# Fetching the rows of two expert tables in turn, and making a block's weights ahead of a later block's selection

## The chip, the cores and the metric

One core of a Trainium2 chip runs one inference step of a small diffusion backbone. The metric is the device time of one execution in microseconds (us). The engines have the profile's names: PE (matrix multiply), DVE (vector), ACT (scalar functions), POOL (here it only issues row fetches), SP (issues the other loads).

## The reference, cut to what matters

384 tokens of width 1024 (128 context tokens, "prompt", and 256 noisy ones, "sample") pass two layers. Layer 0 mixes with an RG-LRU, layer 1 with gated linear attention (GLA). After either comes PEER, a mixture of 16384 tiny experts for each layer, which is where most of the time goes:

```python
def peer(xm, wq, k1, k2, u_tab, v_tab):
    ...
    v1, i1 = lax.top_k(s1, PEER_TOPK)          # 16 of 128 keys, in 8 heads
    v2, i2 = lax.top_k(s2, PEER_TOPK)
    cand = (v1[..., :, None] + v2[..., None, :]).reshape(T, PEER_HEADS, -1)
    cid = (i1[..., :, None] * PEER_NKEYS + i2[..., None, :]).reshape(T, PEER_HEADS, -1)
    sc, pos = lax.top_k(cand, PEER_TOPK)       # 16 experts a head and token
    eid = jnp.take_along_axis(cid, pos, axis=-1)
    gate = jax.nn.softmax(sc, axis=-1)
    ...
        ub = jnp.take(u_tab, eb, axis=0)
        act = jax.nn.gelu(jnp.einsum('td,thkd->thk', xb, ub).astype(jnp.float32))
        vb = jnp.take(v_tab, eb, axis=0)
        return jnp.einsum('thk,thkd->td', (gb * act).astype(vb.dtype), vb)
```

Everything is fp32. For each token and head, 16 rows of 4 KB are taken from the first table (u) and dotted with the token, and 16 rows of the second table (v) are summed with weights gate x gelu(dot).

## The kernel before, in words

The kernel is written with explicit semaphores: each engine runs its own instruction list in order, and every wait is placed by hand or by a table.

**Blocks and rows.** PEER is cut into 48 blocks of 128 tokens and one head: for layer 0 sixteen sample blocks (numbers 0 to 15) and eight prompt blocks (16 to 23), for layer 1 the same (24 to 39, 40 to 47). A block has 16 fetches of each table. One fetch is one `indirect_dma_start` on POOL: it takes 128 table rows of 4 KB, one for each token, to one slot of a ring (512 KB). Below, "row" means such a fetch. The ring of the first table, `ubuf`, has US = 8 slots, that of the second, `vbuf`, VS = 12.

**What happens to a row.** DVE multiplies a first-table row with the tokens and sums it to one column of `dots` (line 1331, a "dot"); this frees the slot (`u_free`). After 16 dots DVE makes the inner value of the gelu (1337 to 1339), ACT its tanh (669), and DVE the weights `wts` (1345 to 1351). ACT turns each column of weights to a diagonal matrix (677), and PE multiplies that with the second-table row and adds to PSUM (974); this frees the slot (`v_free`).

**Selection.** DVE also selects the 16 experts of a block two blocks ahead: `row_tops` (the 16 best of either 128 keys) and `choose` (16 of the 256 sums, and their row numbers `idx`, with a flag at line 1177 on which POOL waits). In a block the order on DVE is: 16 dots, inner value, `row_tops(g + 2)`, weights, `choose(g + 2)`.

**POOL's queue.** The order is written out in two loops. A fetch of the first table waits until the dot eight rows earlier has freed its slot, one of the second until PE has used the row twelve earlier:

```python
            for g, (layer, h, t) in enumerate(BLOCKS):
                ...
                for j in range(TOPK):
                    n = g * TOPK + j
                    if n >= US:
                        pool.wait_ge(u_free, n - US + 1)
                    pool.indirect_dma_start(
                ...
                for j in range(TOPK):
                    n = g * TOPK + j
                    if n >= VS:
                        pool.wait_ge(v_free, n - VS + 1)
```

**The mixers between.** Sample tokens finish layer 0's PEER with block 15, prompt tokens with block 23, so the sample's GLA mixer of layer 1 runs beside the prompt's blocks 16 to 23, and the prompt's mixer beside blocks 24 to 39. The mixers are cut into stages on PE, ACT and DVE. The table `AT` says for each engine and stage after which row (PE: 16 places a block; ACT: 18; DVE: 20) the stage is inserted into the engine's list: a string of turns (S sample, P prompt, Q the PEER queries and scores, T early selections) and a list of places. Slabs of GLA weights (1 MB) come on SP's queue through two buffers. A stage that waits holds up everything behind it on its engine, the rows too.

Of the kernel before, what the change touches and what calls it, by code (L numbers as in the profile page):

```python
# [30 lines left out]
US, VS, DS = 8, 12, 8  # L31
# [39 lines left out]
class Stream:  # L71


    def __init__(self, tag, w, a, n, rot, rot_end):
# [36 lines left out]
        for step in plan:  # L111
# [18 lines left out]
        "QQQQQQQQQQQQSSSSSSSSSSSSSSSSSSSSSSSSSSSSSSSSSSSSSSSSSSSSSSSSSSSSSSSSSSSSSSSSSSSSSQQQQQQQQPPPPPPPQPQP"  # L130
        "PPPPPPPPPPQPPQPPPPPPPPPPPPPPPQPPQPPPPPQPQPPQQQQQQQQQQSSSSQSQQQQQPPP",
# [8 lines left out]
    "ACT": (  # L140
        "SQQQQQQQQQQQQSSSSSSSSSSSSSSSSSSSSSSSSSSSSSSSSSSSSSSSSSSSPQQQQQQQPPPPPPPPQQPPPPPPPQQPPPPPQQPPPPQPQPPP"
        "PQQQQQQQQQQSSQSSSQSQQQQQPPPP",
# [54 lines left out]
def build(nc, x_t, pos_t, vecs, ident_d, mask_d, iota_d, keys_t, ada_w, peer_wq, peer_u, peer_v, rg_w_in,  # L197
          rg_wa, rg_wi, rg_w_out, gla_w_in, w_alpha, state_gla, gla_w_out, y_t, st_rg, st_gla):
    ctx = ExitStack()
    with ctx:  # L200
# [235 lines left out]
        def _(pool):  # L436
# [7 lines left out]
            for g, (layer, h, t) in enumerate(BLOCKS):  # L444
                if t == 0:
                    pool.wait_ge(sem("idx_p"), PH * layer + h + 1)
                else:
                    pool.wait_ge(sem("idx_s"), 2 * PH * layer + 2 * h + t)
# [1044 lines left out]
```

## Time and profile before

| | us |
|---|---|
| three runs, median (lowest to highest) | 2939.15 (2932.97 to 2952.03) |
| the profiled execution, its own time | 2934.96 |
| its span, first to last instruction | 2933.2 |
| PE busy | 2168.3 |
| POOL busy | 1634.3 |
| DVE busy | 1585.9 |
| ACT busy | 538.7 |

The profile is of one execution. Busy time is the time in which an engine works on instructions; idle time stands in front of the instruction that it had to wait for, with what ended the wait. The mean granted clock of PE was 0.862 of full speed. The lines that the prediction rests on come below in numbered groups.

### The profile page before, as it was taken

What the parts mean: (1) busy time and instruction counts of PE and PEld (TensorE: products, weight loads), DVE (VectorE), ACT (ScalarE), POOL (GpSimd) and SP (SyncE); (2) the same over time, 40 slices, a digit from 0 to 9 for tenths busy, and PEclk for the clock granted to TensorE, in tenths of its full rate; (3) what the DMA queues carried; (4) which work ended last, traced back from release to release, by engine and by line L of the source; (5) the groups of instructions that cost most, each with busy time, mean ns of one, the idle gap of its engine ahead of it and who ended that gap; (6) DMA issues with size and microseconds to landing.
All of it is one profiled execution on the core that took longest, in us unless ns stands there. A gap on an engine that the chain in (4) does not pass through costs nothing.

```text
span 2933.2 us, 22324 instructions
## 1 busy us (share of the span) xinstructions
PE 2168.3 (74%) x6996; PEld 1147.8 (39%) x6996; DVE 1585.9 (54%) x3991; ACT 538.7 (18%) x1376; POOL 1634.3 (56%) x1543
## 2 busy tenths in 40 slices
PE   6989667687774747988796697867957576558666
PEld 2545333233332324856442265334524233223323
DVE  3253667666767545164525445665564774466553
ACT  2432111111110113221211122111211111111111
POOL 0000767675767764053567554767575767475664
PEclk9999888898897878988898798888978787778888
DMA  9990989999999996476799788989898999799996
GB/s 307 311 326 16 372 337 361 357 387 339 366 367 361 360 368 237 142 281 225 270 364 379 288 325 315 362 307 347 316 371 311 370 361 363 271 335 345 348 385 245
DMA packets 352933, 938.66 MB, mean 320 GB/s; under 512 B 32369, under 2 KB 155505, under 8 KB 352305
## 3 DMA queue, kind: packets, MB, share of 16 engines
q0 software_dynamic: 221184, 805.40, 73.0%
q1 hardware_dynamic: 123184, 125.32, 13.2%
q10 hardware_dynamic: 8448, 6.51, 0.7%
q8 instruction: 58, 0.95, 0.1%
q14 instruction: 59, 0.48, 0.0%
HBM read 934.49 MB, written 2.63 MB: 319 GB/s over the span
## 4 chain that ended last, share of the span: by engine, by line
PE 34%; another core or an unknown queue 16%; POOL 16%; DMA 12%; issue 12%; DVE 9%; ACT 1%; ACTq 1%; SPq 0%; DVEq 0%; POOLq 0%
PE psum L974 18%; POOL big L454 13%; DMA big<-in_peer_u,idx 4%; PE psum L859 4%; DVE big L1331 3%; POOL big L461 3%; PE psum L797 3%; PE psum L818 3%; DMA big<-in_gla_w_in 2%; DMA big<-in_peer_wq 2%; DMA big<-in_peer_v,idx 2%; PE psum L899 1%; DMA big<-in_ada_w 1%; PE psum L762 1%
## 5 line engine op out<-in xcount | busy, mean ns | idle before, releaser
L974 PE MATMUL psum<-big,diag 128*128 128x512 f32 x3072 | 1435.7, 627 | 485.8 <-issue 244.1
L1331 DVE SCALAR_TENSOR_TENSOR big<-big 128x1024 f32<-128x1024 f32 x768 | 929.9, 1225 | 605.2 <-DMA big<-in_peer_u,idx 526.5
L454 POOL DMA_INDIRECT big<-in_peer_u,idx x768 | 859.4, 1119 | 594.7 <-DVE flag L1177 287.5
L461 POOL DMA_INDIRECT big<-in_peer_v,idx x768 | 770.8, 1004 | 676.8 <-PE psum L974 424.4
L974 PEld LDWEIGHTS psum<-big,diag 128*128 128x128 f32 x3072 | 611.7, 202 | 1264.9 <-issue 1262.8
L677 ACT ACTIVATE diag<-ident,wts 128x128 f32<-128x128 f32 x768 | 273.6, 395 | 914.1 <-PE psum L974 531.9
L818 PE MATMUL psum<-big 128*128 128x384 f32 (+2 forms) x768 | 186.1, 405 | 55.3 <-DMA big<-in_peer_wq 41.6
L818 PEld LDWEIGHTS psum<-big 128*128 128x128 f32 x768 | 136.6, 206 | 112.6 <-DMA big<-in_peer_wq 47.2
L859 PE MATMUL psum<-big 128*128 128x256 f32 (+1 forms) x768 | 142.0, 347 | 42.9 <-issue 19.9
L859 PEld LDWEIGHTS psum<-big 128*128 128x128 f32 x768 | 127.0, 206 | 60.6 <-issue 48.7
L669 ACT ACTIVATE tanh<-inner 128x16 f32<-128x16 f32 x48 | 10.3, 214 | 703.5 <-DVE inner L1339 389.4
L797 PE MATMUL psum<-big 128*128 128x384 f32 x384 | 130.2, 496 | 7.2 <-DVE big L1411 5.2
L797 PEld LDWEIGHTS psum<-big 128*128 128x128 f32 x384 | 72.6, 193 | 61.6 <-issue 11.4
L1194 DVE SCALAR_TENSOR_TENSOR xT<-psum,mods,xT 128x256 f32<-128x256 f32 (+1 forms) x48 | 16.9, 410 | 121.3 <-PE psum L869 98.6
L525 ACT ACTIVATE big<-psum 128x384 f32<-128x384 f32 (+2 forms) x48 | 18.2, 384 | 276.7 <-PE psum L818 187.7
L762 PE MATMUL psum<-big,cond 128*2 128x256 f32 x768 | 52.1, 393 | 19.7 <-DMA big<-in_ada_w 19.7
L1331 DVE DVE_READ_ACCUMULATOR big<-big 128x1 f32 x768 | 62.7, 82 | 0.0
L830 PE MATMUL psum<-big 128*128 128x128 f32 x192 | 28.9, 293 | 40.1 <-ACT big L525 32.6
L1246 DVE COPY big<-psum 128x512 f32<-128x512 f32 (+1 forms) x8 | 4.5, 556 | 96.7 <-PE psum L899 69.7
L869 PE MATMUL psum<-ident,big 128*128 128x128 f32 x48 | 10.2, 395 | 61.7 <-ACT big L568 61.7
L899 PE MATMUL psum<-big 128*128 128x256 f32 x192 | 44.1, 390 | 10.2 <-DMA big<-in_gla_w_in 10.0
L830 PEld LDWEIGHTS psum<-big 128*128 128x128 f32 x192 | 26.8, 204 | 50.0 <-issue 49.2
(182 smaller groups left out, 1306.5 us busy)
## 6 DMA issues: line engine op xcount, KB each, us to landing
big<-in_ada_w SPq DMA_DIRECT2D x48, 1024.0 KB, 8.4
big<-in_peer_wq SPq DMA_DIRECT2D x24, 1024.0 KB
big<-in_gla_w_in SPq DMA_DIRECT2D x24, 1024.0 KB
big<-in_peer_u,idx POOLq DMA_INDIRECT x768
big<-in_peer_v,idx POOLq DMA_INDIRECT x768
big<-in_rg_w_in SPq DMA_DIRECT2D x8, 1024.0 KB, 12.1
big<-in_gla_w_out SPq DMA_DIRECT2D x8, 1024.0 KB
big<-in_rg_w_out SPq DMA_DIRECT2D x4, 1024.0 KB, 8.3
```

What stands on the lines that cost most here:

```text
L454: pool.indirect_dma_start(ubuf[n % US], None, u_rows, bass.IndirectOffsetOnAxis(ap=rows[:, j:j + 1], axis=0)).then_inc(u_in[n % US], 16)
L461: pool.indirect_dma_start(vbuf[n % VS], None, v_rows, bass.IndirectOffsetOnAxis(ap=rows[:, j:j + 1], axis=0)).then_inc(v_in[n % VS], 16)
L525: act.activation(qT[w][half], bank[6 + half][:, 0:width], ACT.Copy).then_inc(sem("q_ev"), 1)
L677: act.activation(diag[n % DS][:, :], ident[:, :], ACT.Copy, scale=wts[g % 3][:, j:j + 1]).then_inc(sem("diag_ready"), 1)
L762: mm = pe.matmul(out[32 * s:32 * s + 2, o:o + SW], cond[:, c, :], slab[SLOT[k]][:, c, :], start=False, stop=(c == C - 1), skip_group_check ...
L797: mm = pe.matmul(out, slab[SLOT[k]][:, c, (n % 2) * P:(n % 2 + 1) * P], rhs[:, c, :], start=(c == 0), stop=(c == C - 1))
L818: mm = pe.matmul(bank[6 + half][:, 0:width], weights[:, c, half * P:(half + 1) * P], rhs[:, c, :], start=(c == 0), stop=(c == C - 1))
L830: mm = pe.matmul(bank[6 + half][:, t * P:(t + 1) * P], qT[w][half][:, t * P:(t + 1) * P], table[:, o:o + NK], start=True, stop=True)
L859: mm = pe.matmul(out[:, j * n:(j + 1) * n], weights[:, c, j % 2 * P:(j % 2 + 1) * P], rhs[:, c, :], start=(c == 0), stop=(c == C - 1), ski ...
L899: mm = pe.matmul(out[:, t * DV:(t + 1) * DV], s.hT[:, c, t * P:(t + 1) * P], weights[:, c, :], start=(c == 0), stop=(c == C - 1), skip_gro ...
L974: mm = pe.matmul(acc[t][:, half * 512:(half + 1) * 512], diag[n % DS][:, :], vbuf[n % VS][:, half * 512:(half + 1) * 512], start=False, st ...
L1331: dve.scalar_tensor_tensor(ubuf[n % US], ubuf[n % US], 1.0, x, ALU.mult, ALU.mult, accum_out=dot[:, j:j + 1]).then_inc(u_free, 1)
```

## The change

Both rings get 10 slots, in place of 8 for the first table and 12 for the second. POOL's queue first takes all 16 rows of the first table for block 0; then, row for row, a row of the second table for block g and one of the first table for block g + 1. On DVE the weights of a block are made directly after its inner value, and `row_tops` of the later block comes behind them. The factor 0.5 of the gelu goes into the dot, so that the two steps ahead of the last one of the weights (scale by the reciprocal sum, multiply by the dots) become one instruction. The places in `AT` are new throughout: on PE the sample's GLA projections, which stood together behind one row (place 268), are now spread over places 267 to 284, and the steps after them over 294 to 321 (before 277 to 304); on DVE the sample's state steps, which stood in one place (379), are spread over 397 to 409; the prompt's stages are spread likewise.

```diff
-US, VS, DS = 8, 12, 8
+US, VS, DS = 10, 10, 8
...
-            for g, (layer, h, t) in enumerate(BLOCKS):
-                if t == 0:
-                    pool.wait_ge(sem("idx_p"), PH * layer + h + 1)
-                else:
-                    pool.wait_ge(sem("idx_s"), 2 * PH * layer + 2 * h + t)
-                rows = idx[kept(g)]
+
+            def first_table(g, j):
+                n = g * TOPK + j
+                if j == 0:
+                    layer, h, t = BLOCKS[g]
+                    if t == 0:
+                        pool.wait_ge(sem("idx_p"), PH * layer + h + 1)
+                    else:
+                        pool.wait_ge(sem("idx_s"), 2 * PH * layer + 2 * h + t)
+                if n >= US:
+                    pool.wait_ge(u_free, n - US + 1)
+                pool.indirect_dma_start(
+                    ubuf[n % US], None, u_rows,
+                    bass.IndirectOffsetOnAxis(ap=idx[kept(g)][:, j:j + 1], axis=0)).then_inc(u_in[n % US], 16)
+
+            def second_table(g, j):
+                n = g * TOPK + j
+                if n >= VS:
+                    pool.wait_ge(v_free, n - VS + 1)
+                pool.indirect_dma_start(
+                    vbuf[n % VS], None, v_rows,
+                    bass.IndirectOffsetOnAxis(ap=idx[kept(g)][:, j:j + 1], axis=0)).then_inc(v_in[n % VS], 16)
+
+            for j in range(TOPK):
+                first_table(0, j)
+            for g in range(NBLK):
                 for j in range(TOPK):
...
+                    second_table(g, j)
+                    if g + 1 < NBLK:
+                        first_table(g + 1, j)
...
-                act.activation(tanh[g % 2][:, :], inner[g % 2][:, :], ACT.Tanh, scale=GELU_C
+                act.activation(tanh[g % 2][:, :], inner[g % 2][:, :], ACT.Tanh, scale=2 * GELU_C
...
-                    dve.scalar_tensor_tensor(ubuf[n % US], ubuf[n % US], 1.0, x, ALU.mult, ALU.mult,
+                    dve.scalar_tensor_tensor(ubuf[n % US], ubuf[n % US], 0.5, x, ALU.mult, ALU.mult,
                                              accum_out=dot[:, j:j + 1]).then_inc(u_free, 1)
...
-                link(dve.tensor_scalar(inn[:, :], inn[:, :], 0.044715, 1.0, ALU.mult, ALU.add))
+                link(dve.tensor_scalar(inn[:, :], inn[:, :], 4 * 0.044715, 1.0, ALU.mult, ALU.add))
                 dve.tensor_tensor(inn[:, :], inn[:, :], dot[:, :], ALU.mult).then_inc(sem("inner_ready"), 1)
                 stages(slot + 17)
-                if look:
-                    row_tops(ahead)
-                stages(slot + 18)
                 dve.wait_ge(sem("exp_ready"), g + 1)
                 link(dve.reciprocal(rz[:, :], esum[r][:, :]))
-                link(dve.tensor_scalar(sc[r][:, :], sc[r][:, :], rz[:, 0:1], 0.5, ALU.mult, ALU.mult))
-                link(dve.tensor_tensor(sc[r][:, :], sc[r][:, :], dot[:, :], ALU.mult))
+                link(dve.scalar_tensor_tensor(sc[r][:, :], sc[r][:, :], rz[:, 0:1], dot[:, :], ALU.mult, ALU.mult))
                 dve.wait_ge(sem("tanh_ready"), g + 1)
                 if g >= 3:
                     dve.wait_ge(sem("diag_ready"), (g - 2) * TOPK)
                 dve.scalar_tensor_tensor(wts[g % 3][:, :], tanh[g % 2][:, :], 1.0, sc[r][:, :], ALU.add, ALU.mult
                                          ).then_inc(sem("w_ready"), 1)
+                stages(slot + 18)
+                if look:
+                    row_tops(ahead)
                 stages(slot + 19)
```

## Rows read from the trace of the kernel before

**Rows 1.** The page: span, and the queue of the row fetches.

```profile
span 2933.2 us, 22324 instructions
...
q0 software_dynamic: 221184, 805.40, 73.0%
```

**Rows 2.** The page's groups: out<-in, count | busy us, mean ns | idle before.

```profile
L974 PE MATMUL psum<-big,diag 128*128 128x512 f32 x3072 | 1435.7, 627 | 485.8 <-issue 244.1
L1331 DVE SCALAR_TENSOR_TENSOR big<-big 128x1024 f32<-128x1024 f32 x768 | 929.9, 1225 | 605.2 <-DMA big<-in_peer_u,idx 526.5
L454 POOL DMA_INDIRECT big<-in_peer_u,idx x768 | 859.4, 1119 | 594.7 <-DVE flag L1177 287.5
L461 POOL DMA_INDIRECT big<-in_peer_v,idx x768 | 770.8, 1004 | 676.8 <-PE psum L974 424.4
```

**Rows 3.** POOL's waits over the span: us, times, longest.

```profile
POOL big L461 <- PE psum L974: 424.4, 171, 82.9
POOL big L454 <- DVE flag L1177: 287.5, 3, 286.8
...
POOL big L454 <- DVE big L1331: 76.4, 13, 13.4
POOL big L461 <- remote: 63.1, 31, 5.3
```

**Rows 4.** Stretches: length; busy PE, PEld, DVE, ACT, POOL; clock, DMA share, GB/s.

```profile
291.00:1076.00 785.00, 562.64 (x1318) 257.67 (x1316) 528.15 (x1467) 112.87 (x334) 547.97 (x525) 0.85 0.95 360
1076.00:1554.00 478.00, 392.82 (x1456) 260.96 (x1456) 204.50 (x412) 102.25 (x219) 215.28 (x194) 0.88 0.73 262
1554.00:1646.00 92.00, 60.63 (x128) 26.07 (x128) 40.80 (x78) 12.54 (x38) 65.10 (x67) 0.81 0.97 373
1646.00:2128.00 482.00, 376.64 (x1344) 219.51 (x1344) 267.40 (x696) 98.23 (x252) 290.89 (x256) 0.87 0.88 321
2128.00:2516.00 388.00, 262.60 (x692) 126.81 (x692) 228.21 (x598) 54.57 (x172) 268.40 (x255) 0.83 0.95 358
2516.00:2907.00 391.00, 247.09 (x624) 116.96 (x625) 211.01 (x527) 58.71 (x178) 242.64 (x243) 0.80 0.90 336
...
820.00:840.00 20.00, 18.33 (x43) 7.79 (x41) 7.74 (x13) 1.20 (x3) 15.02 (x17) 1.00 1.03 412
...
1180.00:1240.00 60.00, 60.00 (x279) 52.82 (x278) 13.64 (x12) 11.17 (x10) 0.00 (x0) 1.00 0.50 157
```

**Rows 5.** POOL's timeline, the longest wait for a ring slot: start, length.

```profile
1244.54 0.95 POOL L461 DMA_INDIRECT big<-in_peer_v,idx  x1 [82.92 <-PE psum L974]
```

**Rows 6.** Timeline of block 10: issues that begin inside a dot.

```profile
793.47 1.99 POOL L454 DMA_INDIRECT big<-in_peer_u,idx  x1 [0.30 <-issue]
794.57 1.22 DVE L1331 SCALAR_TENSOR_TENSOR big<-big 128x1024 f32<-128x1024 f32 x1
...
795.72 1.22 DVE L1331 SCALAR_TENSOR_TENSOR big<-big 128x1024 f32<-128x1024 f32 x1
795.76 1.99 POOL L454 DMA_INDIRECT big<-in_peer_u,idx  x1 [0.30 <-issue]
```

**Rows 7.** Timeline of block 11: its first fetch and dot, and issues beside dots.

```profile
825.85 0.94 POOL L454 DMA_INDIRECT big<-in_peer_u,idx  x1 [0.30 <-issue]
...
832.04 1.28 DVE L1331 SCALAR_TENSOR_TENSOR big<-big 128x1024 f32<-128x1024 f32 x1 [12.56 <-DMA big<-in_peer_u,idx]
...
833.31 0.94 POOL L454 DMA_INDIRECT big<-in_peer_u,idx  x1 [0.31 <-issue]
833.33 1.24 DVE L1331 SCALAR_TENSOR_TENSOR big<-big 128x1024 f32<-128x1024 f32 x1
```

**Rows 8.** DVE's timeline of block 10, from the last dot to the flag.

```profile
809.68 0.17 DVE L1337 TENSOR_TENSOR inner<-dots 128x16 f32<-128x16 f32 x1
...
813.33 0.17 DVE L1351 SCALAR_TENSOR_TENSOR wts<-tanh,sc 128x16 f32<-128x16 f32 x1
...
819.42 0.06 DVE L1177 MEMSET flag<- 128x1 f32 x1
```

More of the change, by code:

```diff
@@ L129 @@
     "PE": (
-        "QQQQQQQQQQQQSSSSSSSSSSSSSSSSSSSSSSSSSSSSSSSSSSSSSSSSSSSSSSSSSSSSSSSSSSSSSSSSSSSSSQQQQQQQQPPPPPPPQPQP"
-        "PPPPPPPPPPQPPQPPPPPPPPPPPPPPPQPPQPPPPPQPQPPQQQQQQQQQQSSSSQSQQQQQPPP",
[8 rows of a table removed]
-    "ACT": (
-        "SQQQQQQQQQQQQSSSSSSSSSSSSSSSSSSSSSSSSSSSSSSSSSSSSSSSSSSSPQQQQQQQPPPPPPPPQQPPPPPPPQQPPPPPQQPPPPQPQPPP"
-        "PQQQQQQQQQQSSQSSSQSQQQQQPPPP",
[6 rows of a table removed]
+        "QQQQQQQQQQQQSSSSSSSSSSSSSSSSSSSSSSSSSSSSSSSSSSSSSSSSSSSSSSSSSSSSSSSSSSSSSSSSSSSSSQQQQQQQQPPPPPPPQQPP"
+        "PPPPPQQPPPPPPPPPPPPPPPPPPPPPPPPPPPQQPPPPPQQQQQQQQQQQQSSSSQQSQQQQPPP",
[8 rows of a table added]
+    "ACT": (
+        "SQQQQQQQQQQQQSSSSSSSSSSSSSSSSSSSSSSSSSSSSSSSSSSSSSSSSSSSPQQQQQQQPPPPPPPQPQPPPQPPQPPPPPPPPPPQQPPPPPPQ"
+        "QQQQQQQQQQQSQQSSSSSQQQQQPPPP",
[6 rows of a table added]
          864]),
@@ L443, in _ @@
             pool.wait_ge(sem("h_ready"), 32)
-            for g, (layer, h, t) in enumerate(BLOCKS):
-                if t == 0:
-                    pool.wait_ge(sem("idx_p"), PH * layer + h + 1)
-                else:
-                    pool.wait_ge(sem("idx_s"), 2 * PH * layer + 2 * h + t)
-                rows = idx[kept(g)]
-                for j in range(TOPK):
-                    n = g * TOPK + j
-                    if n >= US:
-                        pool.wait_ge(u_free, n - US + 1)
-                    pool.indirect_dma_start(
-                        ubuf[n % US], None, u_rows,
-                        bass.IndirectOffsetOnAxis(ap=rows[:, j:j + 1], axis=0)).then_inc(u_in[n % US], 16)
-                for j in range(TOPK):
-                    n = g * TOPK + j
-                    if n >= VS:
-                        pool.wait_ge(v_free, n - VS + 1)
-                    pool.indirect_dma_start(
-                        vbuf[n % VS], None, v_rows,
-                        bass.IndirectOffsetOnAxis(ap=rows[:, j:j + 1], axis=0)).then_inc(v_in[n % VS], 16)
+            def first_table(g, j):
[21 more added lines that the diff above has]
+            for g in range(NBLK):
+                for j in range(TOPK):
+                    second_table(g, j)
+                    if g + 1 < NBLK:
+                        first_table(g + 1, j)
         @block.scalar
```

38 rows, old and new, of the table AT are left out of this document.

## The prediction

> **What bounds the kernel now.** I read the page's groups first, then POOL's waits, then the stages, and only then single instructions. The groups [rows 2] name two candidates. PE spends 1435.7 us on the weighted rows of the second table, 1.87 us a row; POOL spends 859.4 + 770.8 us on issuing the 1536 row fetches, and idles 594.7 + 676.8 us in front of them. Of that idle time 287.5 us lie ahead of the first fetch and 424.4 + 76.4 + 63.1 = 563.9 us are waits for a free ring slot [rows 3]; the remaining 420 us are the 0.30 us step in front of nearly every issue [rows 7]. So from 291 us to 2907 us POOL is either issuing (some 80% of the time) or waiting for a slot, and it is never idle for another reason. The fetches are one queue in program order, so this ledger is the time of the main loop.
>
> The ledger by stage, from the six stretches of [rows 4]: an issue costs 0.94 us when nothing disturbs it [rows 7], plus 0.30, so 32 of them (one block) cost 39.7 us. What a stretch has beyond 1.24 us times its count is disturbance of the issue (POOL's busy time less 0.94 times the count) or a stall.
> - A, 291 to 1076: 525 issues (16.4 blocks), 47.8 us a block: 39.7 + 3.3 slow + 4.8 stall.
> - B, 1076 to 1554, in which the sample's second mixer runs: 194 issues, 204 us of stall.
> - C, 1554 to 1646: 67 issues, 44 us a block, 1.0 of it slow.
> - D, 1646 to 2128, the prompt's mixer: 256 issues, 114 us of stall, 6.3 us slow a block.
> - E, 2128 to 2516: 255 issues, 48.7 us a block, 3.6 slow. F, 2516 to 2907: 243 issues, 51.5 us a block, 1.9 slow.
>
> Is a transfer limit close behind? The fetches move 805.40 MB [rows 1], 16.78 MB a block; the best stretches move 412 GB/s at a share of 1.03 [rows 4], so a block alone needs 40.7 us. With the other loads, the DMA time of a stage is its length times its share: A 0.95 x 785 = 746 us, and at 1.03 it could not be under 724. The same for C, D, E, F: 87, 412, 358, 342. In B PE is the floor instead, with 392.8 us busy of 478 [rows 4].
>
> **What the change does to each.**
> *Order of the fetches.* Before, the queue was sixteen of the first table, sixteen of the second; the thirteenth of the second waits until PE has used the block's first row, which needs the block's weights, which need all sixteen dots. Everything of the next block is queued behind it. After, row j of the second table stands beside row j of the next block's first table, and either ring has 10 slots. The second table's eleventh row is then 21 issues (26 us) behind the last row on which its weights depend. That row lands 6.2 us after its issue starts [rows 7], its dot takes 1.2 [rows 7], the weights follow within 4 [rows 8], and a row of PE 1.9 [rows 2]: 13 us, so 13 us are spare. The next block's eleventh first-table row waits for a dot that starts after the choice of a later block: 6.2 + 1.2 + 9.7 (from the first step after the dots to the flag, [rows 8]) + 1.2 = 18 us against 27. So in plain blocks neither wait should bind, and I leave 0.5 us a block of the 4.8 for the odd late row. The same 32 fetches are issued; nothing is added.
>
> *Weights ahead of the selection.* The row tops lie between the inner value and the weights; both together take 3.65 us from 809.68 to 813.33 [rows 8]. Moving them and merging two 16-element operations brings the weights at most 3 us earlier. The merged step (a few tenths of a us of DVE) is worth nothing by itself, since DVE waits for rows; if that cover were gone it would be 0.2 us in each of 48 blocks, 10 us. The new place adds one wait: DVE now stands until the tanh is back, with the row tops queued behind it, and POOL's next index behind them. ACT's tanh is short and the spare 9 us above cover it; in the mixer stages, where ACT can be late, it may cost something, which I leave in those stages' own range.
>
> *The disturbed issue.* This is the term that decides the plain blocks. Where a fetch is issued just after a dot has begun (795.76 against 795.72), the issue lasts 1.99 us and ends 0.8 us after that dot's end; the next starts 2.29 us after, two dots later, and meets the same thing again [rows 6]. Where issue and dot begin together the issue takes 0.94 and the dots merely stretch to 1.28 and 1.24 [rows 7]. Before, only the first table's issues run beside dots. After, all 32 do. The bounds a block: 1.0 us, as in stage C, and 16 x 1.05 = 16.8 us, every dot delaying one issue by the most that is seen. My value: the choice holds the dots back 9.7 us, so about four rows wait, and with those in flight some 6 dots run back to back; at one issue per two dots that is 3 issues late by 1.05, 3.1 us. The other 10 dots start when their row lands; a random phase would cost half a dot (0.6), a favourable one nothing; 0.3 each, 3.0 us. Together 6.1, close to what stage D pays.
>
> The Trainium skill, "SBUF — State Buffer", section "SBUF: two separate sides", says that a VectorE instruction with two SBUF inputs and a GpSimd instruction that reads SBUF exclude one another for a whole instruction, whichever starts first. The late issues agree with it in one direction [rows 6]; the undisturbed pairs [rows 7] show that the lock is not held for the whole issue. By the rule taken strictly each dot would cost one issue between nothing and its full 1.22 us, at the mean 9.8 us a block in place of 6.1, and the sum would be 2922 us; the slower rival below is this with more than the mean.
>
> *Plain blocks* after: 39.7 + 6.1 + 0.5 = 46.3 us, above the transfer floor of A (724 / 16.4 = 44.1). A 760 (-25), C 97 (+5), E 369 (-19), F 7.6 x 46.3 + 15 for the final transposes of the sample rows, inside which DVE waits, 366 (-25): -64 us.
>
> *Stage B.* The longest stall, 82.9 us [rows 5], is PE: it works through the projections without a pause (60 of 60 us, DMA at 0.50, [rows 4]). The new order of PE puts two or three weighted rows between pairs of slabs, so the fetches go on under the projections; the work of PE stays. At best 85 us, to PE's floor. But the steps after them hold PE at row 299 until DVE is some 20 to 26 rows further on, which is about the most that the rings allow (26), and there each further row costs an issue and 6.2 us of landing, one after the other. I take half: -40. *Stage D*: between 412 and 482; DMA is shared with slabs and the order is again spread; half: -35. Start and end (291 and 27 us) have the same chain before and after, the last sixteen rows of PE behind the last weights: nothing.
>
> Sum: -64 - 40 - 35 = -139. The profiled execution took 2934.96 us, 0.14% under the median of 2939.15, so **2796 us**, 4.8% less.
>
> **The rivals.**
> *It reaches the floors.* If dots and issues fall into step as in [rows 7], each stage ends on DMA or PE: -61 in A, -5, -70, -30, -49, and -85 in B, 300 together: 2635 us. For it: DMA at 0.95 in A is near. Against: stage D, where most dots meet issues, pays 6.3 us.
> *Nothing is gained.* If all 16 dots run back to back against the issues (8 issues late by 1.05, 8.4 us), a block costs 48.6 us, which is the mean of A, C, E and F now (1656 us for 34.1 blocks); with a quarter of the gain in B and D, 2916 us. For it: the ring waits that vanish may only have been standing in for disturbed issues. Also here: the queue is one, so a stop of PE in the mixers now stops the first table after ten rows of the second, as it did after twelve.
> *Slower: dots shut POOL out.* Place: the plain blocks. Price: a delay for each dot, with two issues now offered to each. It decides from the point where 34.1 blocks lose the 75 us won in B and D: 48.6 + 2.2 = 50.8 us a block, 10.6 us of delay, 0.66 us a dot. At 0.85 us a dot a block takes 39.7 + 13.6 + 0.5 = 53.8 us: +177 - 75, 3037 us. For it: late issues come in runs, as in [rows 6]. Against: the dots fill only 929.9 / 48 = 19.4 us of a block [rows 2], and pause for 9.7 of it.
> *The change doesn't do what it says*: the weights are not early enough and the second table still stalls at its eleventh row. The 13 us spare speak against it in plain blocks; it would look like the rival without gain.
>
> **How the numbers follow.** Forecast (2735 to 2870) 0.48; floors 0.22; nothing gained 0.15; slower 0.15. A change under 1% can't be told from none here (the three runs before differ by 0.65%). Faster by over 1% means under 2910: nearly all of the first two and a third of the third, 0.74; within 1% 0.13; slower 0.13. Leaving out the best part of the floors and the worst of the slower cases, the range is 2650 to 2960.
>
> **What would show it.** POOL's waits for PE and for the dots should fall from 564 us to about 300, nearly all of that left in B and D. The means of the two fetch groups should rise from 1119 and 1004 ns towards some 1130 each, the second table's most. The longest single stall should be well under 80 us, and DMA in A reach 0.97 to 1.0. If the means exceed 1270 ns, the slower rival holds; if stalls in A remain at 4 us a block, the slots were not what held it. The forecast fails too if the mixers' new order makes PE and DVE wait on one another, which would stand in B and D alone.

## The result, and the profile after

The changed kernel took 2922.53 us in the median of 20 runs beside 2941.47 us of 20 runs of the kernel before: a ratio of 0.9918, with a 95% interval of 0.9890 to 0.9945. A ratio, here and below, is formed from the runs within 1.5% of the fastest of their kernel, so it can differ from that of the two medians. The forecast was 2796 us. By its time, what came is the rival "nothing is gained", which stood at 2916.

The page's span and groups of the changed kernel answer to [rows 1, 2]; the dot has moved to L1341, the two fetches to L455 and L463, PE's rows to L984:

```profile
span 2908.3 us, 22245 instructions
...
L984 PE MATMUL psum<-big,diag 128*128 128x512 f32 x3072 | 1495.0, 628 | 392.6 <-DMA big<-in_peer_v,idx 245.3
L1341 DVE SCALAR_TENSOR_TENSOR big<-big 128x1024 f32<-128x1024 f32 x768 | 914.3, 1223 | 668.1 <-DMA big<-in_peer_u,idx 587.0
L455 POOL DMA_INDIRECT big<-in_peer_u,idx x768 | 856.6, 1115 | 676.7 <-DVE flag L1187 290.8
L463 POOL DMA_INDIRECT big<-in_peer_v,idx x768 | 892.3, 1162 | 454.2 <-PE psum L984 232.5
```

POOL's waits over the span, beside [rows 3]:

```profile
POOL big L455 <- DVE flag L1187: 290.8, 1, 290.8
POOL big L463 <- PE psum L984: 232.5, 122, 22.1
...
POOL big L455 <- DVE big L1341: 157.8, 19, 18.4
POOL big L463 <- remote: 28.0, 14, 4.9
```

So the second table's wait for PE fell from 424.4 to 232.5 us, as meant; the first table's wait for the dots doubled, from 76.4 to 157.8; and POOL's issues took 1748.9 us in place of 1630.2. Ring waits less 146, issues more 119: 27 us, against 24.9 us by which the span fell.

The stretches, with the columns of [rows 4] and cut at the same six stages:

```profile
295.00:1172.00 877.00, 605.30 (x1305) 242.83 (x1304) 519.38 (x1458) 109.98 (x334) 601.12 (x526) 0.90 0.86 323
1172.00:1570.00 398.00, 358.81 (x1386) 238.09 (x1385) 203.47 (x406) 101.40 (x212) 216.51 (x192) 0.94 0.85 304
1570.00:1665.00 95.00, 79.14 (x199) 36.50 (x197) 40.48 (x75) 13.73 (x42) 72.51 (x66) 0.96 1.03 396
1665.00:2112.00 447.00, 368.79 (x1321) 219.01 (x1322) 260.07 (x686) 102.19 (x254) 295.22 (x256) 0.90 0.93 343
2112.00:2512.00 400.00, 291.46 (x720) 125.39 (x718) 224.08 (x594) 53.01 (x172) 284.99 (x256) 0.91 0.93 353
2512.00:2885.00 373.00, 270.44 (x643) 114.28 (x644) 200.18 (x511) 59.86 (x184) 278.60 (x242) 0.93 0.93 350
```

Against the forecast of each stage: B 398 (438 forecast), C 95 (97), D 447 (447), F 373 (366). A took 877 where 760 was forecast, and E 400 where 369 was; A is even 92 us longer than before. The plain blocks (A, C, E, F) miss by 153 us and B gives 40 back, 113 over the six. Of A's waits 113.4 us, in nine waits, are the first table's eleventh row that waits for a dot; in E and F together it is 44.4 us, in ten:

```profile
POOL big L455 <- DVE big L1341: 113.4, 9, 18.4
...
POOL big L455 <- DVE big L1341: 30.2, 5, 8.9
...
POOL big L455 <- DVE big L1341: 14.2, 5, 6.2
```

The longest of them follows block 9. VectorE's timeline there, then POOL's (start, length, operation, and in brackets the idle time before it; DVE_READ_ACCUMULATOR and the steps without a pause are left out):

```profile
819.32 0.17 DVE L1357 SCALAR_TENSOR_TENSOR wts<-tanh,sc 128x16 f32<-128x16 f32 x1
...
821.83 0.29 DVE L1141 MAX8 v<-work 128x8 f32<-128x128 f32 x1 [0.71 <-DVE v L1141]
823.26 0.09 DVE L1144 MATCH_VALUE_LOAD i12u<-v,work 128x8 f32 x1 [1.14 <-issue]
...
824.65 0.09 DVE L1144 MATCH_VALUE_LOAD i12u<-v,work 128x8 f32 x1 [1.03 <-issue]
...
830.28 0.42 DVE L1161 TENSOR_TENSOR cand<-v 128x256 f32<-128x256 f32 x1 [5.26 <-remote]
...
831.68 0.43 DVE L1133 MAX8 sc<-cand 128x8 f32<-128x256 f32 x1 [0.81 <-issue]
835.26 0.09 DVE L1136 MATCH_VALUE_LOAD posu<-sc,cand 128x8 f32 x1 [3.16 <-remote]
...
838.76 0.43 DVE L1141 MAX8 sc<-onehot 128x8 f32<-128x256 f32 x1 [2.62 <-remote]
...
842.68 0.06 DVE L1187 MEMSET flag<- 128x1 f32 x1
...
850.89 0.06 DVE L1187 MEMSET flag<- 128x1 f32 x1
```

```profile
833.07 0.93 POOL L463 DMA_INDIRECT big<-in_peer_v,idx  x1 [0.30 <-issue]
852.37 1.67 POOL L455 DMA_INDIRECT big<-in_peer_u,idx  x1 [18.36 <-DVE big L1341]
```

Two things are to be seen. There are two flags: the table of places puts the early selection of a later block (the T stages) at the end of every odd block of the first layer, right behind the ordinary one. And the first selection takes 23.4 us, from 819.3 to 842.7, the second, of the same steps, 8.2 us. What makes the first long is seven idle times, 14.7 us together, in front of steps that, by the code, wait for a semaphore of a step before them on the same engine (one of the seven, at 831.68, stands behind a wait for PE too, which had ended by 830.30). The pause between block 9's last dot (its end at 818.30) and the next one (850.87) is 32.6 us; without the seven it is 17.8. The late steps lie where the fetches go out back to back and their rows land (the last issue before POOL's wait starts at 833.07, the last late step at 838.76); the second selection runs while POOL stands still. Late loading of code is not seen: the two queues that carry instructions move nothing between 815 and 855 us.

The other pauses agree. Less its idle times over 0.3 us, the pause behind an odd block up to 13 is 17.5 to 18.3 us, and behind an even one up to 12 it is 9.3 to 9.6; those idle times add 9.3 to 18.4 us to every one of the seven doubled pauses, mainly to the first selection in four of them and to the second in three. Seven of A's nine waits, 98.2 us, stand behind these. The other two, 15.2 us, follow blocks 2 and 4, which have one selection, with 14.2 and 15.6 us of late steps; and no pause in front of the ten waits of E and F holds a T stage. So 59.7 of the 157.8 us stand behind single selections with late steps.

### The profile page after: what moved, and what is told of

Read it like the earlier page. It is cut to its first block, busy times and chain, and to the rows that moved or that the text cites. A ratio compares the mean times of both kernels' runs of the same rounds, so it can differ in the third digit from the quotient of the medians.

```text
span 2908.3 us, 22245 instructions
## 1 busy us (share of the span) xinstructions
PE 2240.7 (77%) x6996; PEld 1118.9 (38%) x6996; DVE 1553.6 (53%) x3943; ACT 539.3 (19%) x1379; POOL 1752.9 (60%) x1543
## 4 chain that ended last, share of the span: by engine, by line
PE 27%; POOL 21%; DMA 15%; issue 13%; DVE 12%; another core or an unknown queue 11%; ACT 1%; ACTq 1%; SPq 0%; DVEq 0%; POOLq 0%
PE psum L984 11%; POOL big L455 11%; POOL big L463 10%; DMA big<-in_peer_v,idx 5%; DMA big<-in_peer_u,idx 5%; PE psum L869 4%; PE psum L807 3%; PE psum L828 3%; DMA big<-in_peer_wq 2%; DVE big L1341 2%; DMA big<-in_ada_w 2%; PE psum L909 1%; PE psum L772 1%; DMA big<-in_gla_w_out 1%
## 5 line engine op out<-in xcount | busy, mean ns | idle before, releaser
L984 PE MATMUL psum<-big,diag 128*128 128x512 f32 x3072 | 1495.0, 628 | 392.6 <-DMA big<-in_peer_v,idx 245.3
L1341 DVE SCALAR_TENSOR_TENSOR big<-big 128x1024 f32<-128x1024 f32 x768 | 914.3, 1223 | 668.1 <-DMA big<-in_peer_u,idx 587.0
L455 POOL DMA_INDIRECT big<-in_peer_u,idx x768 | 856.6, 1115 | 676.7 <-DVE flag L1187 290.8
L463 POOL DMA_INDIRECT big<-in_peer_v,idx x768 | 892.3, 1162 | 454.2 <-PE psum L984 232.5
L984 PEld LDWEIGHTS psum<-big,diag 128*128 128x128 f32 x3072 | 570.8, 197 | 1259.1 <-issue 763.5
L828 PE MATMUL psum<-big 128*128 128x384 f32 (+2 forms) x768 | 209.4, 441 | 137.2 <-ACT big L550 85.9
L828 PEld LDWEIGHTS psum<-big 128*128 128x128 f32 x768 | 151.3, 229 | 204.5 <-issue 148.5
L869 PEld LDWEIGHTS psum<-big 128*128 128x128 f32 x768 | 127.4, 207 | 50.7 <-issue 24.2
L807 PEld LDWEIGHTS psum<-big 128*128 128x128 f32 x384 | 74.7, 197 | 62.4 <-issue 14.5
L1341 DVE DVE_READ_ACCUMULATOR big<-big 128x1 f32 x768 | 62.6, 82 | 0.0
L1141 DVE MAX8 sc<-onehot 128x8 f32<-128x256 f32 x48 | 20.5, 428 | 66.6 <-remote 44.3
L1161 DVE TENSOR_TENSOR cand<-v 128x256 f32<-128x256 f32 x48 | 21.3, 444 | 47.4 <-remote 32.4
L909 PEld LDWEIGHTS psum<-big 128*128 128x128 f32 x192 | 39.7, 208 | 18.2 <-issue 12.2
L1179 DVE TENSOR_TENSOR onehot<-ab,iota 128x512 f32<-128x512 f32 x48 | 33.2, 692 | 15.1 <-DVE ab L1175 7.3
```

The lines of the kernel that those rows point to most:

```text
L455: pool.indirect_dma_start(ubuf[n % US], None, u_rows, bass.IndirectOffsetOnAxis(ap=idx[kept(g)][:, j:j + 1], axis=0)).then_inc(u_in[n % US ...
L463: pool.indirect_dma_start(vbuf[n % VS], None, v_rows, bass.IndirectOffsetOnAxis(ap=idx[kept(g)][:, j:j + 1], axis=0)).then_inc(v_in[n % VS ...
L807: mm = pe.matmul(out, slab[SLOT[k]][:, c, (n % 2) * P:(n % 2 + 1) * P], rhs[:, c, :], start=(c == 0), stop=(c == C - 1))
L828: mm = pe.matmul(bank[6 + half][:, 0:width], weights[:, c, half * P:(half + 1) * P], rhs[:, c, :], start=(c == 0), stop=(c == C - 1))
L869: mm = pe.matmul(out[:, j * n:(j + 1) * n], weights[:, c, j % 2 * P:(j % 2 + 1) * P], rhs[:, c, :], start=(c == 0), stop=(c == C - 1), ski ...
L909: mm = pe.matmul(out[:, t * DV:(t + 1) * DV], s.hT[:, c, t * P:(t + 1) * P], weights[:, c, :], start=(c == 0), stop=(c == C - 1), skip_gro ...
```

## The experiments

The theories, as the expectations number them: **1**, semaphores that come late stretch the selection until ten rows of the ring don't cover the pause; **2**, the doubled selection alone does that; **3**, the gain is lost to issues that last longer beside two-input dots. "Blocks 0 to 15" below is the time from the first dot of block 0 to that of block 16, read from the timeline: 764.8 us before, 838.2 after; blocks 16 to 23 take 568.0 and 493.7. A ratio is to the kernel before, run beside it; kernels without one had a single run, and the 20 runs of the changed kernel lie between 2896 and 2946 us.

**Half rows.** The same fetches, at half the bytes; PE uses the half row for both halves of its sum, and the dot is scaled by 0.05.

```diff
-u_rows = peer_u.rearrange("l n d -> (l n) d")
+u_rows = peer_u.rearrange("l n (two d) -> (l n two) d", two=2)
-ubuf[n % US], None, u_rows,
+ubuf[n % US][:, 0:D // 2], None, u_rows,     # likewise for the second table
```

> The changed kernel, but each fetch brings half a row (2 KB in place of 4 KB a partition), from other rows of the tables; dots and weighted rows keep their widths and work partly on old data, the dot scaled by 0.05. Same number of fetches, same instructions on every engine. Theory 1 (under a saturated DMA the semaphores come late, the selection's chain of short VectorE steps grows from 6 to 9.5 us and the eleventh first-table row waits): with DMA at half its share the choice falls back to 6.0 to 6.5 us, VectorE's gaps inside chained steps fall from 293 to under 60 us, the waits of the first table for dots in the first stage fall from 113 to under 40 us; total 2740 to 2820 us. Theory 2 (the second selection after every odd block is too long by its work alone): these waits stay above 70 us, after odd blocks only; total 2840 to 2900. Theory 3 (issues disturbed by dots eat the gain): fetch means stay at 1115 and 1162 ns and the time stays within 2870 to 2920.

> The kernel before with the same half rows (data and scale of the dot changed in the same way). Its selection is already 6 us long, so Theory 1 expects little in VectorE's gaps (79 us to under 40), and the second table's waits for PE to fall only by what a row lands sooner (about 1 to 3 us a block, 50 to 120 us): 2820 to 2890 us, so that the change is worth 60 to 100 us at half rows in place of 25. Theory 2 and Theory 3: both kernels gain alike, and the difference between the two stays at 20 to 40 us.

Measured: 2760.9 us for the changed kernel, 2858.5 for the one before: between these single runs the change is worth 98 us, in place of 19 between the medians at whole rows. POOL's waits in the first:

```profile
POOL big L463 <- PE psum L984: 164.1, 190, 11.8
POOL big L455 <- DVE big L1341: 27.6, 7, 8.6
```

The idle times over 0.3 us inside the selections, added up over the trace, fell from 293 us to 87 (in the kernel before from 79 to 71), and the choice from 10.6 to 7.5 us. Theory 1 had the total and the waits for dots right, but wanted under 60 us of late steps and a choice of 6.0 to 6.5. POOL's issues grew to 1840.6 us, 92 more. It is theory 1's side; but a half row also lands sooner, and the late steps were not gone, so the pair half_again and half_spread below was added.

**A sum in place of the dot.** One SBUF input in place of two, and one column written in place of a whole row; 1.21 us in place of 1.22.

```diff
-dve.scalar_tensor_tensor(ubuf[n % US], ubuf[n % US], 0.5, x, ..., accum_out=dot[:, j:j + 1])
+dve.tensor_reduce(dot[:, j:j + 1], ubuf[n % US], AX_X, ALU.add)
```

> The changed kernel with each dot replaced by a plain sum over the fetched row: one input from SBUF and no product with the token (so that part of the computation is left out). Theory 3 (what the change wins is lost to fetch issues that last longer beside two-input dots): the fetch means fall from 1115 and 1162 ns to 940 to 1000, some 250 us less on GpSimd, and the total to 2650 to 2750 us. Theories 1 and 2: the issues may get as short, but the time goes into ring waits, since DMA (0.93 in the first stage) and the selection set the pace: 2800 to 2900 us, and the waits for dots and PE grow from 418 us by more than 100.

> The kernel before with the same plain sum in place of the dot (the product with the token is left out). Theory 3: here only the first table's issues were disturbed (1119 ns), so it gains at most 16 x 0.18 us a block, 130 us: 2800 to 2860, and the change is worth over 100 us between the two kernels with sums. Theories 1 and 2: the change stays worth under 50 us between them.

Measured: 2795.4 and 2956.2 us, so that the change is worth 161 us. The fetches of the changed kernel with sums:

```profile
L463 POOL DMA_INDIRECT big<-in_peer_v,idx x768 | 728.1, 948 | 707.9 <-PE psum L984 390.7
L455 POOL DMA_INDIRECT big<-in_peer_u,idx x768 | 731.3, 952 | 597.8 <-DVE flag L1187 287.1
```

The issues are at their undisturbed 0.95 us, so what lengthens them is the dot's instruction; whether by its second input or by the row that it writes, this edit doesn't separate. POOL's busy time falls by 289 us, the ring waits grow from 418 to 608, the span falls by 115. In the kernel before the same edit takes 181 us from POOL and gives nothing: its wait for PE grows from 424.4 to 581.1 us. Neither side has all its numbers. Theory 3 had the issue times and the worth of over 100 us right, but both totals wrong (2795.4 against 2650 to 2750, 2956.2 against 2800 to 2860). Theories 1 and 2 had the growth of the waits right and the first total nearly (2800 to 2900), and were wrong on the worth, which they put under 50 us. The price of the disturbed issue already stands in the forecast (6.1 us a block; 6.4 measured). It is a cost of the new order, and not the one that was missed; the next three runs show that.

**The pause taken apart.** "spread" moves the T stages from slots 40, 80, ... 280 (the ends of blocks 1, 3, ... 13) to 48, 88, ... 288 (behind the eighth dot of the next block), and the query projections that they hold up by four places on PE and up to two on ScalarE. "mid" moves the row tops:

```diff
 for j in range(TOPK):
     ... dot j ...
+    if look and j == 11:
+        row_tops(ahead)
     stages(slot + 1 + j)
 ...
 stages(slot + 18)
-if look:
-    row_tops(ahead)
 stages(slot + 19)
```

> The changed kernel with the early selections of blocks 16 to 22 moved from the end of the odd blocks of layer 0 (where each stands right behind another selection) to the middle of the block after (behind its eighth dot), with the query projections that they hold up moved along by a few places. Same instructions. Theories 1 and 2 (the doubled pause of the dots is longer than the ten rows of the first ring cover): the waits of the first table for dots in the first stage fall from 113 us to under 40, the sixteen first blocks take 765 to 800 us in place of 838, total 2850 to 2885 us. Theory 3 (issues beside dots): waits that vanish come back as longer issues, since the dots then run back to back less often but the same issues stay disturbed: total within 2900 to 2930.

> The changed kernel with the row tops of the selection (MAX8 and its like on the scores, some 3.7 us) moved from the end of the block to between its eleventh and its twelfth dot plus one; the rest of the selection stays. Theory 1 (a chain of short steps that gets long under a saturated DMA, so that its length decides): the pause between the blocks' dots falls by 4 to 8 us, the waits for dots by a third to a half: 2860 to 2895 us. Theory 2 alone: only the odd blocks of layer 0 gain, 7 times 4 to 5 us: 2885 to 2900. Theory 3: no change, 2905 to 2930.

> Both of these edits in one kernel. Theories 1 and 2: the waits of the first table for dots all but vanish (under 40 us of 158), total 2820 to 2865 us. Theory 3: within 2890 to 2930.

Measured: spread 2835.8 us, ratio 0.9708 [0.9619, 0.9797]; mid 2833.1, 0.9717 [0.9621, 0.9812]; both 2781.5, 0.9545 [0.9452, 0.9638]. Blocks 0 to 15 take 772.3, 813.8 and 775.5 us. POOL's waits of spread, then those of mid for dots, and then of spread_mid with its groups of fetches:

```profile
POOL big L463 <- PE psum L984: 252.6, 131, 19.6
...
POOL big L455 <- DVE big L1341: 66.1, 16, 9.0
```

```profile
POOL big L455 <- DVE big L1343: 72.0, 9, 12.1
```

```profile
POOL big L463 <- PE psum L984: 227.7, 130, 16.6
...
POOL big L455 <- DVE big L1343: 31.1, 9, 8.9
POOL big L463 <- remote: 23.1, 10, 5.2
POOL big L463 <- DVE big L1343: 4.0, 1, 4.0
```

```profile
L455 POOL DMA_INDIRECT big<-in_peer_u,idx x768 | 886.2, 1154 | 553.6 <-DVE flag L1187 291.2
L463 POOL DMA_INDIRECT big<-in_peer_v,idx x768 | 866.6, 1128 | 446.0 <-PE psum L984 227.7
```

In spread_mid POOL's issues are as long as in the changed kernel (1752.8 against 1748.9 us), the ring waits fell from 418 to 286 us, and the span by 127: the gain is in the waits. The first table's wait for dots is 66.1 us with the second selection moved away, close to the 59.7 that stood behind single selections, 72.0 in mid, and 31.1 with both. Theory 3 expected 2890 or more for all three and falls as the explanation of the miss. On this chip the kernel before was faster, too (2925.0 us); by their ratios the three would be at 2856, 2858 and 2808 us beside the 2941.47 above. So spread is where theories 1 and 2 put it; mid is at the lower edge of theory 1's range and well under the 2885 to 2900 of theory 2 alone; and the two together are some 12 us better than expected. Fewer steps were late, too (145 us in place of 293).

The time of spread_mid is near the forecast, but its parts are not. Blocks 0 to 15, at 775.5 us, are no shorter than in the kernel before (764.8), where the forecast had 25 us off in A. What it wins lies in blocks 16 to 23 (478 us in place of 568) and 24 to 39 (809 in place of 871). Its stretch that answers to A is as long as A was, with the same share of DMA:

```profile
295.00:1080.00 785.00, 579.40 (x1297) 242.06 (x1296) 503.84 (x1438) 111.81 (x334) 583.31 (x517) 0.92 0.95 357
```

**The weights alone.**

> The kernel before (its order of fetches, rings of 8 and 12, places) with one part of the change: the block's weights are made ahead of the selection, with the two 16-element operations merged. As the prediction has it, the weights come 3 us earlier and shorten the second table's wait at its thirteenth row in the plain blocks by up to that: 0 to 60 us off, 2880 to 2940. The rival, that the wait for the tanh costs as much as the move gives: 2935 to 2955. If it alone reaches 2920, the new order of the fetches is worth nothing as it stands.

Measured: 2915.6 us, ratio 0.9944 [0.9890, 0.9999]; the wait of L461 for PE fell from 424.4 to 332.6 us, and that for the dots rose from 76.4 to 115.1:

```profile
POOL big L461 <- PE psum L974: 332.6, 139, 78.5
...
POOL big L454 <- DVE big L1331: 115.1, 18, 13.3
```

Alone it wins 0.6%, with an interval that all but touches 1, where the whole change wins 0.8% (1.2% in the comparison further below). The intervals overlap: that the new order, with its rings and places, adds anything as it stands is not shown.

**The old order with the pause taken apart, and the new order with the old places.** The first is weights_only with the edits of spread_mid (T stages on the same slots, PE's query places moved by four); the second puts the table of the kernel before into the changed one.

> The kernel before (sixteen of the first table, then sixteen of the second; rings of 8 and 12; its places) with the weights ahead of the selection and with both edits of the run spread_mid: early selections in the middle of the block after, row tops behind the twelfth dot. Theory A (the new order lets the next block's fetches pass the wait for the weights, and its gain was only covered by the pause of the dots): the old order gains little from shorter pauses, its second table still waits for the weights: 2880 to 2915 us, at least 80 us over spread_mid. Rival B (the pause of the dots is all there was, and either order gains alike): 2780 to 2850 us.

> The changed kernel with the table of places of the kernel before (when PE, ScalarE and VectorE turn to the mixers and the query projections); the order of the fetches, the rings and the early weights are those of the change. If the new places are what made the sample's mixer 59 us shorter (blocks 16 to 23: 552 to 494 us), these blocks take 530 us or more and the total is 2945 to 2985 us. If the order of the fetches did it, the total stays within 2900 to 2940 us; the first sixteen blocks stay at 820 to 850 us in either case.

Measured: 3014.7 us, ratio 1.0150 [1.0072, 1.0229], and 3033.4 us, 1.0340 [1.0287, 1.0393]. The first ratio rests on two of six runs, of 2964.4 and 2994.2 us; the trace is of one of 3011.2. POOL's waits of the old order taken apart, then of the new order at the old places:

```profile
POOL big L461 <- PE psum L974: 450.6, 166, 78.2
...
POOL big L454 <- DVE big L1333: 94.6, 14, 13.3
```

```profile
POOL big L455 <- DVE big L1341: 362.8, 38, 41.1
...
POOL big L463 <- PE psum L984: 158.9, 108, 74.6
```

The old order loses with the edit that wins 4% in the new one: the row tops now stand ahead of the last four dots, the weights come later, and the second table's thirteenth row waits for them (332.6 to 450.6 us). So the two orders want opposite things of VectorE: the old one the weights early, the new one short pauses. Theory A expected no gain there (2880 to 2915) and met a loss. The old places cost the new order more than the 2945 to 2985 expected: blocks 16 to 23 take 532.7 us, near the threshold of 530, but 24 to 31 also 39 us more than in the changed kernel, and blocks 0 to 15 take 862.3, over the 820 to 850 expected in either case. The expectation's "552" for the kernel before was misread; it is 568.0, so the new places and order together win 74 us there, not 59. The old order with the new places was not run, so how much of this the places would win by themselves stays open.

**Further apart, and a shorter ring.** "all_mid" puts the row tops behind the eighth dot, the choice behind the twelfth, the T stages behind the fourth; "ring_9_10" sets `US, VS = 9, 10` in the changed kernel.

> The changed kernel with the selection taken apart further: row tops behind the eighth dot, the choice behind the twelfth, the early selections of blocks 16 to 22 behind the fourth dot of the even blocks, so that only the weights stand between two blocks' dots. If the pause of the dots still costs ring waits (31 us for the first table in spread_mid) and the rest is late weights behind the choice, 2745 to 2780 us. If spread_mid already stands at the transfers (DMA at 0.94 to 0.98 in its plain stages): within 1% of it, 2770 to 2800 us.

> The changed kernel with 9 rows in the first table's ring in place of 10. The dose of Theory 1 and 2: a pause that ten rows do not cover costs one row more, two issues of 1.15 + 0.3 us, 2.9 us each time: the 23 waits of the first table for dots and about as many that ten rows just covered, some 45 times 2.9: +60 to +130 us, 2980 to 3050 us, nearly all in the plain blocks. If the waits have to do with issues or places instead: within 20 us of the changed kernel.

Measured: 2800.7 us, ratio 0.9545 [0.9493, 0.9597], the same as spread_mid: taking the pause apart further won nothing more. The shorter ring: 2929.0 us, 0.9999 [0.9964, 1.0035], and its wait for dots:

```profile
POOL big L455 <- DVE big L1341: 182.4, 20, 17.9
```

That is 0.8% over the change, some 24 us (by the intervals 10 to 37), and 182.4 us of waits for dots in place of 157.8. The expectation, 60 to 130, missed; the other side, within 20, is nearer. The number of waits stayed at 20 (19 in the changed kernel, where the expectation has 23), so no waits came up that ten rows had just covered. Blocks 0 to 15 take 857.9 us, 20 more, as seven odd blocks at 2.9 us would have it; but another execution of the changed kernel (change_again) took 852.9 there, so that is no support. A ring that fills earlier also ends the run of issues earlier, and with it the late steps (262 us in place of 293); that this is why the dose is small was not tested.

**What the doubled pause costs by itself.** Half rows again, with and without the edit of spread, and the changed kernel and spread_mid on one chip.

> The run half_after once more, timed in rounds beside half_spread (half rows, the dot scaled by 0.05): 2750 to 2775 us, with the waits of the first table for dots at 20 to 40 us.

> Half rows (as in half_after: each fetch brings half a row, other rows of the tables, the dot scaled by 0.05) together with the early selections in the middle of the block after (as in spread). If the doubled pause and the late semaphores cost only together (two selections of 8.6 us each just fit under the ten rows' cover when their steps are not late), moving the second selection gives little at half rows: within 25 us of half_again. If the doubled pause costs by itself, it gives as much as at whole rows, 60 to 90 us: 2670 to 2700 us.

> The changed kernel itself, on the chip on which spread_mid is timed again: 2905 to 2930 us, a ratio to the kernel before of 0.989 to 0.996. All theories expect the same; it gives the distance between the two on one chip.

> The run spread_mid once more, beside the changed kernel: 2775 to 2815 us, a ratio to the kernel before of 0.945 to 0.964, and 100 to 140 us under the changed kernel, if the pause of the dots is what ate the change's gain.

Measured: half_again 2760.3 us, 0.9479 [0.9436, 0.9522]; half_spread 2733.5, 0.9387 [0.9357, 0.9417]. The edit is worth 27 us at half rows (12 to 42 by the intervals), just over the 25 of the first reading and far from the second's 60 to 90, and at whole rows (0.9918 to 0.9708) some 60 (34 to 89). Block 5's pause in half_again:

```profile
573.53 0.17 DVE L1357 SCALAR_TENSOR_TENSOR wts<-tanh,sc 128x16 f32<-128x16 f32 x1
...
581.86 0.06 DVE L1187 MEMSET flag<- 128x1 f32 x1
...
588.45 0.43 DVE L1141 MAX8 sc<-onehot 128x8 f32<-128x256 f32 x1 [2.31 <-remote]
...
590.55 0.17 DVE L1173 TENSOR_SCALAR abu<-posu 128x16 uint32<-128x16 uint32 x1 [1.15 <-DVE posu L1144]
...
594.75 0.69 DVE L1182 TENSOR_TENSOR onehot<-onehot,i 128x512 f32<-128x512 f32 x1 [2.10 <-issue]
...
597.58 0.06 DVE L1187 MEMSET flag<- 128x1 f32 x1
```

At half rows the first selection is on time (8.3 us from weights to flag) and only the second is late (15.7 us). With the second moved away every pause of the odd blocks is 9 us, in place of 24 to 27, and the late steps sum to 11 us in place of 95. So the two causes work together: two selections on time would just fit, late steps in either make the pause too long, and a longer pause gives them more room. Some 27 of spread's 60 us are left where the first selection is on time; by the intervals the two worths are not clearly apart, and a half row also lands sooner, so this split is rough.

On one chip: the change 2873.8 us, 0.9884 [0.9843, 0.9926], where 2905 to 2930 and 0.989 to 0.996 were expected (the kernel before took 2912.6 on it); spread_mid 2776.5, 0.9551 [0.9523, 0.9580], as expected. The version with the pause taken apart beats the kernel before by 4.5% and the change by 97 us.

## Why the prediction was wrong, step by step

- **What bounds the kernel: right.** The ledger of issues and ring waits carries the comparisons above to within some 15 us.
- **Order of the fetches, second table: right.** In stage A the wait of L463 for PE is 11.4 us; the 13 us spare were there.
- **Order of the fetches, first table: the step that failed.** "The next block's eleventh first-table row waits for a dot that starts after the choice of a later block: ... 18 us against 27", and with it "0.5 us a block" for the odd late row; measured in A, 124.8 us of waits for dots and PE, 7.6 us a block. Two errors are in it. The 9.7 us of one selection were taken for every block, though the table of places, which the diff shows, sets a T stage at the end of each odd block of the first layer: with it the pause is 17.8 us, and 6.2 + 1.2 + 17.8 + 1.2 = 26.4 against 27, with nothing spare. And the selection's length was read in the kernel before, where the queue mostly stands in the second table's wait while it runs; in the new order fetches go out throughout, and the choice (from cand to the flag) took 10.6 us in the mean in place of 6.8. By that sum the doubled selection alone would have been at the edge; late steps with one selection cost 59.7 us of waits, 44.4 of them in E and F (31 and 7 us over the forecast); together they gave pauses of 27 to 36 us after the odd blocks, and 98.2 us of waits. What makes the steps late stays open.
- **Plain blocks: their gain did not come even without the stalls.** The forecast had 46.3 us a block, 760 in A; spread_mid takes 48.5 us a block in blocks 0 to 15, with 52.7 us of ring waits left there (21.4 for dots, 31.3 for PE and the rest) at a DMA share of 0.95, and all_mid 757.1 us in all, 8 under the kernel before. So that spread_mid comes near the forecast's time is in part luck: it wins more beside the mixers than was forecast, and nothing in the first layer's plain blocks, where 25 us were forecast. Whether the transfers hold these blocks at 0.95, under the 1.03 that the floor of A assumed, stays open: at half the bytes (half_spread, a share of 0.63) they still take 763.2 us, but with longer issues.
- **Weights ahead of the selection: not contradicted.** Alone, in the old order, it measures 0.9944 [0.9890, 0.9999]; what it gives inside the new order was not measured. The new wait for the tanh cost nothing that the runs show.
- **The disturbed issue: right.** 6.1 us a block forecast, (1748.9 - 1536 x 0.94) / 48 = 6.4 measured; means of 1115 and 1162 ns against "some 1130 each". The Trainium skill, "SBUF — State Buffer", section "SBUF: two separate sides", names two SBUF inputs of a VectorE instruction as a condition of the lock; the sum with one input, at 948 and 952 ns, agrees, though it also writes less. The full delay of the strict rule (9.8 us) did not come.
- **Stages B, C, D: B 40 us better than forecast, C and D as forecast.** By old_places most of these gains need the new places: with the old ones blocks 16 to 23 gain 35 us over the kernel before, and 24 to 39 lose 24.
- **The ring waits** were forecast at about 300 us, nearly all in B and D; they were 418, with 130 in A, and 286 in spread_mid.
- **The rival** "nothing is gained" had the time right and the cause wrong: it wanted 8.4 us of disturbance a block. The issues were as forecast; the stalls were not.

## What to carry to other kernels

When two rings share one queue, what each must cover is the longest pause of its consumer, so add up every step that any table or schedule puts in that pause, block by block, and not in a typical block. A duration read while the queue stands still may not hold once the queue runs: look for the same steps in a stretch where it does run. And after a reordering ask where the slack now lies: work that had to stand behind the weights in the old order could be moved between the dots in the new one, and most of the 4.5% came only with that. Last, a time that agrees with a forecast proves little until its stages agree too.

## What the runs showed of the hardware

A step that waits for the semaphore of a step before it on its own engine followed within 0.04 us in most cases; here it could come up to 5.3 us late. The selections' steps that wait for nothing else, in the trace of the changed kernel, had a mean idle time before them of at most 0.13 us when up to six fetches had been issued in the last 10 us, 0.19 when seven had, and 0.90 when eight or more had (eight is one each 1.24 us, the undisturbed rate). At half rows (half_again) it was 0.05 at seven and 0.33 at eight; in the kernel before 0.17 and 0.37, and 93 steps stood at eight in place of 258. So it goes with an unbroken run of fetches, and less so at half the bytes; but with sums in the old order (reduce_before) 118 steps at eight had 0.11, so the run of issues is not all of it.

The late steps keep a rhythm. In the trace of half_again 588.45, 590.55, 591.28, 591.95, 594.75 and 596.15 lie within 0.03 us of multiples of 0.70 us apart; over that trace 63 of the 65 distances between late steps less than 6 us apart lie within 0.05 us of a multiple of 0.70, in the changed kernel 128 of 149 (by chance it would be one in seven). What serves the semaphores in that rhythm stays open.
